# Gate/up bias of an expert as two 64-row products on the two row halves of the array

## The chip, the cores and the metric

The kernel runs on one core of a Trainium2 chip. The metric is the device time of one execution in microseconds (us), lower is better; the figure given for a kernel is the median of its runs.

## The reference

One layer of a decoder trunk is computed for 512 prompt tokens and 64 sample tokens (T = 576 in all): a combined input projection, a Mamba-2 branch, a latent attention branch, a gated merge, a layer norm, and then a mixture of 32 experts with the top 4 chosen for each token. The change lies in the experts:

```python
def expert_block(arg):
    xb, e = arg                                   # 128 rows of tokens, one expert
    gu = xb @ w_gu[e] + b_gu[e]                   # D_MODEL=1024 -> 2*D_FF=2048, gate and up interleaved
    g = jnp.minimum(gu[:, ::2], SWIGLU_LIMIT)
    u = jnp.clip(gu[:, 1::2], -SWIGLU_LIMIT, SWIGLU_LIMIT)
    h = (u + 1.0) * (g * jax.nn.sigmoid(SWIGLU_ALPHA * g))
    return h @ w_dn[e] + b_dn[e]
```

All inputs and outputs are float32.

## The kernel before

The program is a sequence of stages, each a block in which every engine has its own instruction list and engines meet through semaphores. `stage_choose` (up to about 1242 us of the profiled execution) does the output projection, the first layer norm and the routing. `stage_experts_combine` then runs the experts.

**An item** is one expert with up to 128 of its token rows. The first four items are written out, the others run in a loop of two per turn; a further loop for experts with more than 128 rows stands behind it and has nothing to do in the profiled execution. Each item reads 12 pieces of weights of 1 MiB (slots 0 to 3 for the first half of the gate/up matrix, 4 to 7 for its second half, 8 to 11 for the down matrix) into a ring of 8 raw buffers.

**Precision by splitting.** A float32 matrix is split into a high part in the type fp32r (ScalarE copies it, `high`, L2798) and a low part (VectorE subtracts, `low`, L2853). A product then needs three fp32r matmuls: x_hi by w_hi, x_hi by w_lo, x_lo by w_hi. `w_hi` and `w_lo` have 4 slots each. The order is: DMA brings a raw piece, ScalarE waits until TensorE has used the slot four pieces back (`w_used`) and writes `w_hi`, VectorE writes `w_lo`, TensorE uses both.

**TensorE's list in an item** (`run` in the tensor block). For each half h of the gate/up output: four pieces of 12 matmuls, all 128 rows by 128 columns with 512 moving columns (L2708), into PSUM banks 2h and 2h + 1, then `add_bias` (L2714), whose last matmul increments `gu_ready`. Then the down product, four more pieces, 48 matmuls. Between them stand 16 transposes (L2702) which turn the hidden rows and the token rows of the next item. So an item has 144 product matmuls, 4 bias matmuls and 16 transposes.

**The bias** is added by a matmul too. `pick[:, par, :]` is a one-hot over the experts, copied by GpSimd from column `K_PICK + e` of the constants and broadcast to 128 columns. `sb.b_all` is a table of 128 rows by 3072 columns: rows 0 to 31 hold the high parts of the biases of the 32 experts, rows 32 to 63 the low parts, rows 64 to 127 are zero in the gate/up columns 0 to 2047 (GpSimd writes them, L2161). One half needs two matmuls of 128 rows and 512 columns, one for each bank, with the same stationary operand. The down bias columns, with a second copy of the high part in rows 64 to 95, are used once at the very end (`down_bias`, L2771).

**After the bias** of a half ScalarE takes the sigmoid (L2807), VectorE clips and multiplies (L2862, L2863, L2866) and writes `hid`. TensorE needs the first half of `hid` for the transposes `turn(U_H0)`, behind the second piece of half 1, and the second half of it for `turn(U_H1)`, in the middle of the second piece of the down product.

**The set-up of the bias table** is in `stage_choose`: five DMAs of SyncE (L2130 to L2132) into the free room of `xT`, the up bias plus one on GpSimd (L2164), the high parts on ScalarE at the second token tile (L2327, L2328), the low parts on GpSimd (L2166).

Of the kernel before, what the change touches and what calls it, by code (L numbers as in the profile page):

```python
# [8 lines left out]
F32 = mybir.dt.float32  # L9
# [3 lines left out]
ALU = mybir.AluOpType  # L13
ACT = mybir.ActivationFunctionType
AX = mybir.AxisListType.X

P = 128
D = 1024
# [20 lines left out]
FF = 1024  # L39
E = 32  # L40
# [25 lines left out]
K_STRICT = K_TRI + P  # L66
# [15 lines left out]
K_PICK = K_VAL + NT  # L82
# [6 lines left out]
def constants():  # L89
    c = np.zeros((P, K_W), np.float32)  # L90
    r = np.arange(P)[:, None]
    q = np.arange(P)[None, :]
    c[:, K_ID:K_ID + P] = r == q
    c[:, K_TRI:K_TRI + P] = r <= q
    c[:, K_STRICT:K_STRICT + P] = r < q
    c[:, K_ONE:K_ONE + P] = 1
    c[:, K_CAUS:K_CAUS + P] = np.where(q <= r, 0, MASKED)
    l = np.arange(NS)
    same = l[:, None] // TS == l[None, :] // TS
    c[:NS, K_BTRI:K_BTRI + NS] = same & (l[:, None] <= l[None, :])  # L100
    c[:NS, K_BALL:K_BALL + NS] = same
    s = np.arange(NSEQ)
    c[:NS, K_BEND:K_BEND + NSEQ] = l[:, None] == s[None, :] * TS + TS - 1
    c[:NS, K_BROW:K_BROW + NSEQ] = l[:, None] // TS == s[None, :]
    c[:, K_BCOL:K_BCOL + NSEQ * NS] = (s[:, None] == l[None, :] // TS).reshape(1, -1)
    t = np.arange(TS)
    c[:, K_NEW:K_PAIR] = MASKED
    c[:HEADS * TS, K_NEW + NS - TS:K_NEW + NS] = np.where(t[None, :] <= np.tile(t, HEADS)[:, None], 0, MASKED)
    c[:, K_FOLD:K_FOLD + HEADS * TS] = r % (HEADS * TS) == np.arange(HEADS * TS)[None, :]
    c[:, K_SUB] = np.arange(P) % 16  # L110
    c[:NS, K_BMOD:K_BMOD + 4] = l[:, None] // TS % 4 == np.arange(4)[None, :]
    pair = np.zeros((P, NT * TOPK, 2))
    token = np.repeat(r + P * np.arange(NT)[None, :], TOPK, axis=1)
    pair[:, :, 0] = token
    c[:, K_PAIR:K_BASE] = pair.reshape(P, -1)
    c[:, K_BASE:K_BASE + E] = CAP * np.arange(E)
    c[:E, K_CODE:K_CODE + 4] = CAP * np.arange(E)[:, None] + P * np.arange(1, 5)[None, :]
    c[:E, K_CODE + 4] = np.arange(E)
    c[:, K_OVER:K_OVER + 4] = P * np.arange(1, 5)
    c[:, K_ITEM:K_ITEM + NOVF + 2] = np.arange(1, NOVF + 3)  # L120
    c[:, K_IOTA:K_IOTA + P] = q
    c[:, K_VAL:K_VAL + NT] = token[:, ::TOPK] - T
    c[:2 * E, K_PICK:K_PICK + E] = (r % E == np.arange(E)[None, :])[:2 * E]
    return c


# [1939 lines left out]
def stage_choose(nc, io, sb, sem):  # L2066

    with ExitStack() as ctx:
        buf = lambda n, s, d=F32: ctx.enter_context(nc.sbuf_tensor(n, s, d))
        K = sb.const  # L2070
        h, w_raw, w_hi, w_lo = sb.h, sb.w_raw, sb.w_hi, sb.w_lo
        room = sb.xT[:].rearrange("p k t -> p (k t)")
        b_raw = room[0:2 * E, 0:3 * D]
        down_again = room[2 * E:3 * E, 2 * D:3 * D]
        up = b_raw[:, 0:2 * FF].rearrange("p (f t) -> p f t", t=2)
        picks, parts = (room[:, 3 * D + 640 * j:3 * D + 640 * (j + 1)].rearrange("p (k i e) -> p k i e", k=TOPK, i=NT) for j in range(2))
        g_b, b_b = w_raw[4][:, 0, :], w_raw[4][:, 1, :]
        spots = w_raw[5].rearrange("p c n -> p (c n)")[:, 0:LISTED * NT * P].rearrange("p (e i c) -> p e i c", e=LISTED, i=NT)
# [38 lines left out]
        with nc.Block() as block:  # L2117
            @block.sync
            def _(sp):
                for q in (2, 3):  # L2120
                    sp.dma_start(w_out[q], out_piece(io, q)).then_inc(w_in_[q], 16)
                for i in range(NT):
                    sp.dma_start(h[0:ROWS[i], i, :], token_dram(io.xp, io.xs, i)).then_inc(x_in, 16)
                sp.dma_start(g_b, io.g1.broadcast_to((P, D))).then_inc(gb_in, 16)
                sp.dma_start(b_b, io.b1.broadcast_to((P, D))).then_inc(gb_in, 16)
                sp.dma_start(wr[:], io.wr.rearrange("(k p) n -> p k n", p=P)).then_inc(wr_in, 16)
                sp.dma_start(br[:], io.br.broadcast_to((P, E))).then_inc(wr_in, 16)
                sp.wait_ge(wo_low, 2)
                for p0 in (0, E):
                    sp.dma_start(b_raw[p0:p0 + E, 0:2 * FF], io.bgu).then_inc(b_in, 16)  # L2130
                    sp.dma_start(b_raw[p0:p0 + E, 2 * FF:3 * D], io.bdn).then_inc(b_in, 16)
                sp.dma_start(down_again, io.bdn).then_inc(b_in, 16)  # L2132
                sp.wait_ge(zeroed, 3)
                sp.dma_start(io.slots[NEMPTY:NEMPTY + P].unsqueeze(0), empty[0:1]).then_inc(cleared, 16)
                sp.dma_start(io.slots[0:NEMPTY].rearrange("(e j c) a -> e j c a", e=E, c=P),
                             empty[:].unsqueeze(1).broadcast_to((E, CAP // P, P, 2))).then_inc(cleared, 16)
                for rows in (io.y_sum, io.h_rows):
                    sp.dma_start(rows[T:T + P].rearrange("r (q n) -> r q n", n=ZW),
                                 zero.unsqueeze(1).broadcast_to((P, D // ZW, ZW))).then_inc(cleared, 16)
                for s in range(AHEAD):  # L2140
                    sp.wait_ge(wo_low, s + 1)
                    sp.dma_start(w_raw[s], weight_slot(io, 0, s)).then_inc(first_in[s], 16)
                for i in range(NT):
                    sp.wait_ge(done, i + 1)
                    sp.dma_start(io.h_rows[P * i:P * i + ROWS[i], :], h[0:ROWS[i], i, :]).then_inc(stored, 16)
                    sp.wait_ge(raised, i + 1)
                    sp.dma_start(io.y_sum[P * i:P * i + ROWS[i], :], stage[i % 2][0:ROWS[i], :]).then_inc(y_put[i % 2], 16)
                sp.wait_ge(stored, 16 * NT)
                sp.wait_ge(y_put[0], 48)
                sp.wait_ge(y_put[1], 32)  # L2150
                sp.wait_ge(cleared, 16 * 4)

            @block.gpsimd
            def _(pool):
                pool.memset(zero, 0.0).then_inc(zeroed, 1)
                pool.tensor_copy(sb.pair[:], K[:, K_PAIR:K_BASE].rearrange("p (n a) -> p n a", a=2)).then_inc(zeroed, 1)
                pool.memset(empty[:, :, 1], 0.0)
                pool.tensor_scalar(empty[:, :, 0], K[0:E, K_IOTA:K_IOTA + P], float(T), None, ALU.add).then_inc(zeroed, 1)
                pool.wait_ge(zeroed, 3)
                pool.wait_ge(wo_low, 4)  # L2160
                pool.tensor_copy(sb.b_all[2 * E:P, 0:2 * D], K[2 * E:P, K_STRICT:K_STRICT + 1].broadcast_to((P - 2 * E, 2 * D))).then_inc(b_low, 1)  # L2161
                pool.wait_ge(b_in, 80)
                pool.wait_ge(b_low, 1)
                pool.tensor_scalar(up[:, :, 1], up[:, :, 1], 1.0, None, ALU.add).then_inc(b_up, 1)  # L2164
                pool.wait_ge(b_high, 1)
                pool.tensor_tensor(sb.b_all[E:2 * E], b_raw[E:2 * E], sb.b_all[E:2 * E].bitcast(F32), ALU.subtract).then_inc(b_low, 1)  # L2166
                pool.wait_ge(b_low, 2)
                pool.wait_ge(stored, 16 * NT)
                pool.wait_ge(cleared, 16 * 4)
                pool.wait_ge(first_put, 1)  # L2170
                pool.indirect_dma_start(out=x_first, out_offset=None, in_=io.h_rows,
                                        in_offset=bass.IndirectOffsetOnAxis(ap=first_row[:].bitcast(U32), axis=0)).then_inc(x_got, 16)
                pool.wait_ge(x_got, 16)
# [96 lines left out]
            def _(act):  # L2270
# [42 lines left out]
                for i in range(NT):  # L2313
                    if i >= 1:
                        turned_copy(i - 1)
                    if i + 2 < NT:
                        act.wait_ge(mixed, i + 1)
                        merged_high(i + 2)
                    if i == NT - 1:
                        act.wait_ge(mixed, NT)  # L2320
                        expert_high(0)
                    root(i)
                    if i >= 1:
                        raise_rows(i - 1)
                    if i == 1:
                        act.wait_ge(b_up, 1)
                        act.activation(sb.b_all[2 * E:3 * E, 2 * D:3 * D], down_again, ACT.Copy)  # L2327
                        act.activation(sb.b_all[0:2 * E], b_raw, ACT.Copy).then_inc(b_high, 1)  # L2328
                expert_high(1)
                turned_copy(NT - 1)  # L2330
# [177 lines left out]
def stage_experts_combine(nc, io, sb):  # L2508
# [5 lines left out]
    with ExitStack() as ctx:  # L2514
        sem = ctx.enter_context(signals(nc, "experts"))
        buf = lambda n, s, d=F32: ctx.enter_context(nc.sbuf_tensor(n, s, d))
        K = sb.const
# [77 lines left out]
        with nc.Block() as block:  # L2595
# [102 lines left out]
            def _(pe):  # L2698
# [12 lines left out]

                def add_bias(par, bank, row, stop):
                    for c in range(2):
                        mm = pe.matmul(banks[:, bank + c, :], pick[:, par, :], sb.b_all[:, (row + c) * 512:(row + c + 1) * 512], start=False, stop=stop)  # L2714
                    return mm

                def run(it, par):
# [377 lines left out]
```

## Time and profile before

| | |
|---|---|
| median of 3 runs | 2427.85 us (2427.7 to 2431.04) |
| profiled execution | span 2428.8 us, its own time is this span |
| busy in it: TensorE matmul, weight load | 2315.2 us (95%), 1895.8 us (78%) |
| VectorE, ScalarE, GpSimd | 1845.1, 1341.9, 486.6 us |
| experts | from about 1242 us to 2395 us, 32 items |

The profile shows, for each engine, when each instruction started and how long it took; for a TensorE matmul the length includes the time in which it drains while the next is already under way, so the distance from one start to the next tells what a matmul costs in a stream. A group "x2" is two instructions in a row of the same line; its length runs from the first start to the last end.

### The profile page before, as it was taken

How to read it: one execution, taken by the hardware profiler on the slowest of the kernel's cores; microseconds unless marked ns; L12 is line 12 of the kernel's file. 1: busy time of each engine (PE TensorE's matmuls, PEld its weight loads, DVE VectorE, ACT ScalarE, POOL GpSimd, SP SyncE). 2: the span in 40 equal slices, each digit the busy share in tenths (PEclk: the TensorE clock that was granted, in tenths of full speed). 3: DMA queues.
4: the chain of work that ended last, by engine and by line, in shares of the span. 5: the costliest groups of instructions: out<-in, count | busy, mean ns of one | idle time of the engine just before them, and what ended most of it. 6: DMA issues, size and time to landing. Idle time of an engine off the chain costs nothing. (4 is left out here: it accounts for less than half of the span.)

```text
span 2428.8 us, 38736 instructions
## 1 busy us (share of the span) xinstructions
PE 2315.2 (95%) x14529; PEld 1895.8 (78%) x14529; DVE 1845.1 (76%) x2270; ACT 1341.9 (55%) x1470; POOL 486.6 (20%) x414
## 2 busy tenths in 40 slices
PE   8898999999989999998978999999999999999997
PEld 5486656999976667898767888888888888888885
DVE  2575556428778888444478999999999999999997
ACT  1351212314336776322337777777777777777775
POOL 0002220000014444000142222122122212212223
PEclk9997999999989999999979999999999999999999
DMA  5105562424232444433559999999999999999995
GB/s 174 67 1 201 188 218 99 122 54 154 83 86 78 143 133 111 148 122 112 182 165 362 394 394 397 392 382 381 395 382 379 389 391 380 378 395 384 380 386 195
DMA packets 250686, 593.64 MB, mean 244 GB/s; under 512 B 31056, under 2 KB 122577, under 8 KB 245836
## 3 DMA queue, kind: packets, MB, share of 16 engines
q1 hardware_dynamic: 232884, 514.07, 58.0%
q0 software_dynamic: 17680, 77.88, 10.1%
q8 instruction: 84, 1.38, 0.2%
q14 instruction: 38, 0.31, 0.0%
HBM read 553.75 MB, written 38.16 MB: 244 GB/s over the span
## 5 line engine op out<-in xcount | busy, mean ns | idle before, releaser
L2853 DVE TENSOR_TENSOR w_lo<-w_raw,w_hi 128x2048 fp32r<-128x2048 f32 x291 | 658.7, 2288 | 53.6 <-ACT w_hi L2798 49.6
L2798 ACT ACTIVATE w_hi<-w_raw 128x2048 fp32r<-128x2048 f32 x288 | 550.2, 1916 | 117.6 <-PE banks L2708 88.7
L2708 PE MATMUL banks<-w_hi,x_hi 128*128 128x512 f32 x1024 | 320.0, 394 | 3.9 <-DVEq L2898 3.5
L2708 PE MATMUL banks<-w_lo,x_hi 128*128 128x512 f32 x1024 | 316.9, 391 | 0.0
L2708 PE MATMUL banks<-w_hi,x_lo 128*128 128x512 f32 x1024 | 316.3, 390 | 0.0
L2853 DVE TENSOR_TENSOR w_lo<-mergedT,w_hi 128x2048 fp32r<-128x2048 f32 x96 | 220.0, 2292 | 33.1 <-ACT w_hi L2798 31.0
L2708 PEld LDWEIGHTS banks<-w_hi,x_lo 128*128 128x128 f32 x1024 | 192.8, 188 | 41.0
L2708 PEld LDWEIGHTS banks<-w_lo,x_hi 128*128 128x128 f32 x1024 | 192.9, 188 | 40.9
L2708 PEld LDWEIGHTS banks<-w_hi,x_hi 128*128 128x128 f32 x1024 | 190.5, 189 | 42.4 <-DVEq L2898 3.9
L2656 POOL DMA_INDIRECT y_sum<-xT,to_row x31 | 51.0, 1644 | 826.9 <-ACT xT L2835 783.6
L2798 ACT ACTIVATE w_hi<-mergedT 128x2048 fp32r<-128x2048 f32 x96 | 183.9, 1915 | 35.2 <-PE banks L2708 29.9
L2708 PE MATMUL banks<-w_hi,h_hi 128*128 128x512 f32 x512 | 161.6, 397 | 0.9 <-DVE w_lo L2853 0.9
L2708 PE MATMUL banks<-w_lo,h_hi 128*128 128x512 f32 x512 | 158.7, 391 | 0.0
L2708 PE MATMUL banks<-w_hi,h_lo 128*128 128x512 f32 x512 | 157.8, 389 | 0.0
L757 PE MATMUL banks<-keyT,q 32*64 32x256 f32 x2560 | 117.4, 424 | 17.0 <-issue 15.0
L757 PEld LDWEIGHTS banks<-keyT,q 32*64 32x64 f32 x2560 | 79.0, 148 | 49.9 <-issue 43.6
L2708 PEld LDWEIGHTS banks<-w_lo,h_hi 128*128 128x128 f32 x512 | 96.4, 188 | 20.7
L2708 PEld LDWEIGHTS banks<-w_hi,h_lo 128*128 128x128 f32 x512 | 96.2, 188 | 20.8
L2708 PEld LDWEIGHTS banks<-w_hi,h_hi 128*128 128x128 f32 x512 | 93.9, 189 | 19.0 <-DVE w_lo L2853 1.3
L808 ACT ACTIVATE prob<-banks,neg 128x1024 f32<-128x1024 f32 x16 | 17.8, 1114 | 155.9 <-DVE neg L856 155.9
L1175 DVE TENSOR_TENSOR ws_lo<-room,ws_hi 128x1024 fp32r<-128x1024 f32 x22 | 27.0, 1226 | 82.4 <-ACT ws_hi L1153 82.4
L1348 PE MATMUL banks<-xs_hi,ws_hi 128*128 128x288 f32 x384 | 84.3, 301 | 4.0 <-DVE ws_lo L1422 4.0
(539 smaller groups left out, 4743.4 us busy)
## 6 DMA issues: line engine op xcount, KB each, us to landing
w_raw<-in_exp_w_gu SPq DMA_DIRECT2D x196, 1024.0 KB
w_raw<-in_exp_w_down SPq DMA_DIRECT2D x96, 1024.0 KB, 9.8
mergedT<-in_exp_w_gu SPq DMA_DIRECT2D x64, 1024.0 KB
mergedT<-in_exp_w_down SPq DMA_DIRECT2D x32, 1024.0 KB, 9.8
w_x<-in_w_in SPq DMA_DIRECT2D x11, 1024.0 KB, 5.3
xT<-in_w_in SPq DMA_DIRECT2D x9, 1024.0 KB
room<-acs_rows SPq DMA_DIRECT2D x16, 512.0 KB, 4.0
mergedT<-in_state_ssm SPq DMA_DIRECT2D x16, 512.0 KB, 6.5
```

Of the source, the lines that this page charges most:

```text
L757: mm = pe.matmul(banks[64 * c:64 * (c + 1), i, 0:HALF], q4[at, b % 2, j, :], keyT[at, j, c * HALF:(c + 1) * HALF], start=(j == 0), stop=(j ...
L808: act.activation(prob[:, n % 2].rearrange("p (k i x) -> p i k x", k=BLK, i=4), scores_at.rearrange("p i (k x) -> p i k x", k=BLK), ACT.Exp ...
L1175: dve.tensor_tensor(w_lo[:, u % NW], w_raw[u % NR], w_hi[:, u % NW].bitcast(F32), ALU.subtract).then_inc(w_low, 1)
L1348: mm = pe.matmul(banks[:, b + piece, 0:H2], wp[:, c % 2, k, at:at + P], part[:, k, piece * H2:(piece + 1) * H2], start=(k == 0 and wp is w ...
L2656: pool.indirect_dma_start(out=io.y_sum, out_offset=bass.IndirectOffsetOnAxis(ap=to_row[:, par, :].bitcast(U32), axis=0), in_=y_out, in_off ...
L2708: mm = pe.matmul(banks[:, bank + c, :], x[:, k, :], part[:, s % NHI, j, c * 512:(c + 1) * 512], start=start, stop=last)
L2798: act.activation(w_hi[:, s % NHI], raw(s, par), ACT.Copy).then_inc(hi_ready, 1)
L2853: dve.tensor_tensor(w_lo[:, s % NHI], raw(s, par), w_hi[:, s % NHI].bitcast(F32), ALU.subtract).then_inc(lo_ready, 1)
```

## The change

The gate/up bias table is laid out a second time in rows 64 to 127 (rows 64 to 95 high, 96 to 127 low) where there were zeros. The one-hot column of the constants has the pattern in all 128 rows. The two bias matmuls of a half then take 64 rows each: the one for the first bank rows 0 to 63, the one for the second bank rows 64 to 127 of `pick` and of the table. In the set-up, two DMAs of 256 KB are added, the addition of one to the up bias goes over 128 partitions, ScalarE gets one more copy, GpSimd one more subtraction, and GpSimd's writing of zeros is gone.

```diff
-    c[:2 * E, K_PICK:K_PICK + E] = (r % E == np.arange(E)[None, :])[:2 * E]
+    c[:, K_PICK:K_PICK + E] = r % E == np.arange(E)[None, :]
...
         b_raw = room[0:2 * E, 0:3 * D]
+        gu_again = room[2 * E:P, 0:2 * D]
         down_again = room[2 * E:3 * E, 2 * D:3 * D]
-        up = b_raw[:, 0:2 * FF].rearrange("p (f t) -> p f t", t=2)
+        up = room[:, 0:2 * FF].rearrange("p (f t) -> p f t", t=2)
...
                     sp.dma_start(b_raw[p0:p0 + E, 2 * FF:3 * D], io.bdn).then_inc(b_in, 16)
+                for p0 in (2 * E, 3 * E):
+                    sp.dma_start(room[p0:p0 + E, 0:2 * FF], io.bgu).then_inc(b_in, 16)
                 sp.dma_start(down_again, io.bdn).then_inc(b_in, 16)
...
                 pool.wait_ge(zeroed, 3)
-                pool.wait_ge(wo_low, 4)
-                pool.tensor_copy(sb.b_all[2 * E:P, 0:2 * D], K[2 * E:P, K_STRICT:K_STRICT + 1].broadcast_to((P - 2 * E, 2 * D))).then_inc(b_low, 1)
-                pool.wait_ge(b_in, 80)
-                pool.wait_ge(b_low, 1)
+                pool.wait_ge(b_in, 112)
                 pool.tensor_scalar(up[:, :, 1], up[:, :, 1], 1.0, None, ALU.add).then_inc(b_up, 1)
                 pool.wait_ge(b_high, 1)
                 pool.tensor_tensor(sb.b_all[E:2 * E], b_raw[E:2 * E], sb.b_all[E:2 * E].bitcast(F32), ALU.subtract).then_inc(b_low, 1)
+                pool.tensor_tensor(sb.b_all[3 * E:P, 0:2 * D], room[3 * E:P, 0:2 * D], sb.b_all[3 * E:P, 0:2 * D].bitcast(F32), ALU.subtract).then_inc(b_low, 1)
...
                         act.activation(sb.b_all[2 * E:3 * E, 2 * D:3 * D], down_again, ACT.Copy)
+                        act.activation(sb.b_all[2 * E:P, 0:2 * D], gu_again, ACT.Copy)
                         act.activation(sb.b_all[0:2 * E], b_raw, ACT.Copy).then_inc(b_high, 1)
...
                 def add_bias(par, bank, row, stop):
                     for c in range(2):
-                        mm = pe.matmul(banks[:, bank + c, :], pick[:, par, :], sb.b_all[:, (row + c) * 512:(row + c + 1) * 512], start=False, stop=stop)
+                        at = slice(2 * E * c, 2 * E * (c + 1))
+                        mm = pe.matmul(banks[:, bank + c, :], pick[at, par, :], sb.b_all[at, (row + c) * 512:(row + c + 1) * 512], start=False, stop=stop)
                     return mm
```

## Rows read from the trace of the kernel before

**Rows 1.** The page: busy time by engine, share of the span, instructions.

```profile
PE 2315.2 (95%) x14529; PEld 1895.8 (78%) x14529; DVE 1845.1 (76%) x2270; ACT 1341.9 (55%) x1470; POOL 486.6 (20%) x414
```

**Rows 2.** The chain that ended last, in order of time: start, length, what.

```profile
1396.74 17.73 PE banks L2708 x78
...
1432.14 17.73 PE banks L2708 x78
...
2388.12 6.85 PE banks L2708 x30
```

**Rows 3.** One item by windows: length, busy time by engine, granted clock, DMA share, GB/s.

```profile
1432.14:1467.55 35.41, 35.41 (x166) 29.45 (x165) 33.13 (x23) 26.85 (x20) 7.29 (x6) 1.00 1.03 397
```

**Rows 4.** Waits from 1396.74 to 2388: who, for whom, total, times, longest.

```profile
ACT w_hi L2798 <- PE banks L2708: 108.3, 196, 0.8
...
DVE w_lo L2853 <- ACT w_hi L2798: 59.2, 83, 1.4
```

**Rows 5.** Timeline of PE around the bias of a half 0: start, length.

```profile
1449.26 0.62 PE L2708 MATMUL banks<-w_hi,x_lo 128*128 128x512 f32 x2
1449.71 0.61 PE L2714 MATMUL banks<-b_all,pick 128*128 128x512 f32 x2
1450.17 0.62 PE L2708 MATMUL banks<-w_hi,x_hi 128*128 128x512 f32 x2
```

**Rows 6.** Timeline of PE in the scan stage, 128-row fp32r matmuls before 32-row ones.

```profile
788.50 0.39 PE L1689 MATMUL banks<-ws_lo,xs_hi 128*128 128x512 f32 x1
788.73 0.40 PE L1689 MATMUL banks<-ws_hi,xs_lo 128*128 128x512 f32 x1
789.07 1.99 PE L1757 MATMUL banks<-b_of,xend 32*128 32x512 f32 x8
```

**Rows 7.** The same stage, from two pairs of 32-row matmuls back to 128 rows.

```profile
782.22 1.13 PE L1757 MATMUL banks<-b_of,xend 32*128 32x512 f32 x4
783.28 0.50 PE L1689 MATMUL banks<-ws_hi,xs_hi 128*128 128x512 f32 x1
783.62 0.39 PE L1689 MATMUL banks<-ws_lo,xs_hi 128*128 128x512 f32 x1
```

**Rows 8.** Line L1757's matmuls of the whole run: duration ns min/median/max, first and last start.

```profile
L1757 PE MATMUL banks<-b_of,xend x64: 587/587/692, 780.2 to 983.2; 32*128 32x512 f32 x64
```

**Rows 9.** Timeline of PE: four full float32 matmuls of 128 rows, 512 columns.

```profile
2402.46 1.88 PE L2784 MATMUL banks<-h,const 128*128 128x512 f32 x4
2404.18 0.59 PE L2789 MATMUL banks<-xT 128*128 128x512 f32 x1
```

**Rows 10.** Timeline of PE in the scan stage: 128 rows, then 64.

```profile
767.74 0.60 PE L1769 MATMUL banks<-const,y 128*128 128x128 f32 x4
768.26 1.14 PE L1701 MATMUL banks<-xdt,room 64*64 64x64 f32 x16
```

**Rows 11.** Timeline of PE in the third item: its half-1 bias and the turns.

```profile
1354.75 0.62 PE L2714 MATMUL banks<-b_all,pick 128*128 128x512 f32 x2
...
1360.30 1.09 PE L2702 MATMUL banks<-const,xT 128*128 128x128 f32 x8 [0.42 <-DMA xT<-h_rows,from_row]
```

**Rows 12.** Set-up, timeline of ACT.

```profile
1174.48 2.77 ACT L2328 ACTIVATE b_all<-xT 64x3072 fp32r<-64x3072 f32 x1
1179.65 0.60 ACT L2292 ACTIVATE mergedT<-banks 128x512 f32<-128x512 f32 x1 [2.40 <-PE banks L2198]
```

**Rows 13.** Set-up, timeline of POOL.

```profile
1163.69 3.33 POOL L2164 TENSOR_SCALAR xT<-xT 64x1024 f32<-64x1024 f32 x1 [9.04 <-DMA xT<-in_exp_b_down]
1177.34 6.79 POOL L2166 TENSOR_TENSOR b_all<-xT,b_all 32x3072 fp32r<-32x3072 f32 x1 [10.32 <-ACT b_all L2328]
1230.68 1.15 POOL L2171 DMA_INDIRECT xT<-h_rows,first_row  x1 [46.55 <-DVE first_row L2466]
```

**Rows 14.** The hidden rows' last step on DVE, and their turn on PE.

```profile
1464.50 0.69 DVE L2866 SCALAR_TENSOR_TENSOR xT<-xT 128x512 f32<-128x512 f32 x1
...
1466.08 1.47 PE L2702 MATMUL banks<-const,xT 128*128 128x128 f32 x12
```

## Prediction, before the changed kernel was run

> **What bounds the kernel now.** I read the busy times of the page first [rows 1]: TensorE works 95% of the span, the others less, so the question is whether its few gaps or its work set the end. The chain that ended last, in order of time, answers that for the experts [rows 2]: from about 1361 us to 2395 us it is TensorE alone, in pieces of product matmuls that come back every 35.40 us (1396.74, 1432.14). The window of one item shows the same from the other side [rows 3]: TensorE is busy 35.41 of 35.41 us at a granted clock of 1.00. VectorE has 2.3 us to spare in it, ScalarE 8.6. The DMA engines are busy throughout too (share 1.03, 397 GB/s), so it matters who waits for whom [rows 4]: in 28 items ScalarE waited for TensorE before its copies of weights (196 times, 108.3 us) and never for a weight transfer, TensorE for nobody. So a nanosecond more or less in TensorE's list of an item appears in the item, as long as DMA and VectorE keep up.
>
> The work in front is different. The third item waits for the gather of the fourth item's tokens until 1360.30 [rows 11]. Before it the first items wait for weights. So the stream that is bound by TensorE begins behind that turn and holds items 4 to 32: 29 items, 58 halves with a bias each.
>
> **What a bias costs now.** In the stream the last two product matmuls start from 1449.26, the two bias matmuls from 1449.71, the next two products from 1450.17 [rows 5]: 0.91 us for four starts, 0.227 us for each. A bias is two of these, 0.454 us.
>
> **What the change takes away.** Two 64-row matmuls on different row halves and into different banks can run side by side. The nearest row in the trace is line 1757 of the scan stage, pairs of 32-row matmuls in two row groups, into two banks, 512 columns each. Four of them (two pairs) start at 782.22 and the last ends 1.13 us later [rows 7]. Full float32 matmuls of 512 columns start every 0.43 us when they follow each other (2402.46 to 2404.18 is four) [rows 9], so four in a row would last 1.88. They went in pairs. By this row the change saves one of the two, 0.227 us in a half. That those are float32, which stream at 0.43 us and not 0.227, is the weak point of the analogy, and it is rival 2.
>
> **What the change adds.** The array goes from 128 rows to 64 and back, and the same line shows what that costs, in four places:
> - Before the first tiled matmul. Line 1689, fp32r, 128 rows, 512 columns, is the same kind as our products: its starts lie 0.23 apart (788.50, 788.73), but the first tiled one comes 0.34 behind the last (789.07) [rows 6]. That is +0.11.
> - In the first tiled pair. Line 1757's matmul lasts 587 ns in the median, 692 at most [rows 8], and the 1.13 us of rows 7 is 0.53 from the first pair to the second, not 0.43, and 0.59 or so. The weight load is not hidden under the matmul before. That is +0.105.
> - Behind the last tiled pair. From 782.22 to the next untiled start, 783.28, two pairs take 1.06 us [rows 7] instead of 0.86 (two times 0.43 [rows 9]). The excess of 0.20 holds the 0.105 just counted, so +0.095 remains.
> - In the first untiled matmul. It starts at 783.28, the next at 783.62: 0.34 instead of 0.23, and it lasts 0.50 instead of 0.39 [rows 7]. That is +0.105.
>
> Together 0.415 us for a visit to the tiled form. That 64 rows, and not only 32, are such a form is seen at line 1701: four 128-row transposes start at 767.74 and the 64-row matmul behind them at 768.26, 0.52 later [rows 10], where four at their usual 0.11 make 0.44. So the price of going in is paid there also.
>
> The Trainium skill has a rule against this change: "TensorEngine Tiling (Array Packing)", Tiling Modes, Key Properties, says that a change of the tiling mode drains TensorE. The trace agrees, with the 0.34 us above. The page "TensorE: Matmul & The Clock Gate", Part 3, tells the other half: matmuls of different row groups overlap almost entirely, with some 4 ns more for each tile. With that page alone the sum in a half would be a gain of 0.22 us; with both, a loss of the size of the drain less this.
>
> **The sum in a half.** Now, from the start of the last product to the start of the second product behind the bias: 4 times 0.227 = 0.91 us. Then: 0.227 + 0.11, the pair at 0.227 + 0.105 + 0.095, the first product at 0.227 + 0.105, which is 1.09 us. The difference is 0.415 - 0.227 = +0.19 us. Our products last 0.39 where the 788.73 one shows 0.40, so the drain may be a few ns less; I take +0.18. The rows' own spread (0.10 to 0.11 for each of four) gives 0.16 to 0.20.
>
> 58 halves by 0.18 us = +10.4 us.
>
> **What lies off the path.** The bias of the third item, half 1 (1354.75), is before the wait of 0.42 us for the gather [rows 11], which swallows 0.18. In half 0 of that item, and in the first two, TensorE's loss falls into waits for transfers and for VectorE. What hangs on the bias itself moves hardly at all: the last bias matmul ends at +0.11 + 0.105 - 0.227, about 0.01 us earlier than now, so the sigmoid, the gate and `hid` come when they do now, and the turn that needs `hid` comes later. The tighter of the two turns starts at 1466.08, its `hid` is ready at 1465.19 [rows 14]: 0.9 us of cover, which grows. SyncE's loads wait for freed buffers, so they get slower with TensorE and the DMA engines get relief, not load.
>
> The pick on GpSimd has the same shape as before and is ready long ahead.
>
> **The set-up.** ScalarE gets a copy of 64 by 2048. 64 by 3072 takes 2.77 us and ends at 1177.25 [rows 12], so the new one takes some 1.9. ScalarE then waits 2.40 us for TensorE, until 1179.65; it fits with 0.5 us over. Without this cover it would be at most 1.9 us. GpSimd's addition (3.33 us, from 1163.69) goes over 128 partitions, which I cost between 3.33 and twice that, and starts behind 512 KB more of transfers, 1.3 us at the 397 GB/s of rows 3; ScalarE wants it about a microsecond before 1174.48 [rows 12], so even 6.7 us fit. SyncE has two more issues in front of its list, of under a microsecond together; behind them stand the clearing of tables and the first expert's weights, whose users come tens of microseconds later. GpSimd's new subtraction of 32 by 2048 takes two thirds of 6.79 us, 4.5, and ends at about 1189; its next work is at 1230.68 [rows 13]. The zeros that it no longer writes were off the path. I cost the set-up at zero, at most 2 us.
>
> **The forecast.** The span of the profiled execution would go from 2428.8 to 2439.2 us. The runs' median is 2427.85, so 2438.3 us for the changed kernel.
>
> **Rivals.**
> 1. *The pair overlaps and the switch is free for our fp32r products*, for instance because weights of the next form are loaded while the last products stream. Then 58 times 0.227 = 13.2 us are gained: 2414.7 us. For it speaks that everything else in the stream hides its weight loads. This is also what the Trainium skill's page "TensorE: Matmul & The Clock Gate", Part 3, would give, which names no cost of a switch. Against it stands that the fp32r stream of line 1689 paid on both sides [rows 6, 7]. It decides from a switch of under 0.227 us. Chance 0.09.
> 2. *The pair does not overlap*, since two fp32r matmuls at 0.227 us each write two banks at twice the rate that any row here shows. Nothing is saved and the switch is paid: 58 times 0.415 = 24.1 us, 2451.9. Chance 0.10.
> 3. *The switch costs about what the pair saves*, 0.15 to 0.31 us, for instance with one of the four terms hidden. Then the time is within 5 us of before. Chance 0.08; the term that could go is the weight load of the first pair, which two 64-row loads might share otherwise than two 32-row ones.
> 4. *The forecast*: overlap and a full switch. Chance 0.73.
>
> **Range and chances.** This kernel's measurement can tell some 0.2%, 4.9 us. Rivals 2 and 4 are slower by more, 0.83; rival 3 is the same, 0.08; rival 1 faster, 0.09. The likeliest case by itself holds 2436 to 2441 us (0.16 to 0.20 in a half, and up to 2 us of set-up). The range that leaves out only rivals 1 and 3 is 2434 to 2452.
>
> **What the profile of the changed kernel would show.** The period of an item is 35.40 + 0.36 = 35.76 us, and TensorE is still busy all of it. The two bias matmuls start together, within 0.01 us; they last about 0.49 and not 0.39 us. The last product before them is followed 0.33 us later by the pair, the pair 0.42 us later by a product, and that product, 0.50 us long, 0.33 us later by the next. If the pair starts 0.2 us apart, rival 2 holds; if a product of 0.39 us follows the pair after 0.23, rival 1. The experts begin at 1242 us as now. The prediction is wrong if the switch of a 64-row form into whole-column width is cheaper than that of line 1757, if the pair is serial, or if TensorE's loss is caught up by a wait that I have not seen; rows 4 show none.

## The result, and the profile of the changed kernel

The changed kernel takes 2439.68 us in the median of 5 runs (2435.6 to 2443.45), the kernel before 2428.84 us in 5 runs (2427.7 to 2431.04). The ratio is 1.004 with a 95% interval of 1.0029 to 1.0052: slower by 10.8 us (7 to 13 by the interval). The profiled execution has a span of 2436.1 us and a time of 2438.17. The profile says where the loss is: in TensorE's list, at every bias.

The chain that ended last, in order of time (start, length, what), for two items of the changed kernel; it answers to [rows 2]:

```profile
1426.85 17.73 PE banks L2710 x78
1444.58 0.43 PE banks L2717 x2
1445.01 5.67 PE banks L2710 x24
...
1456.61 0.43 PE banks L2717 x2
1457.04 4.31 PE banks L2710 x18
1461.35 1.31 PE banks L2704 x12
1462.66 17.73 PE banks L2710 x78
...
1498.48 17.73 PE banks L2710 x78
...
2393.81 6.85 PE banks L2710 x30
```

It is still TensorE from end to end. Line 2710 is the product (2708 before), 2717 the bias, 2704 the transposes. An item takes 35.81 us (1426.85 to 1462.66 to 1498.48, and to 2393.81 in the mean of 27 items), where it took 35.41 (1396.74 to 2388.12 is 28): +0.41, 0.20 for each bias. One item by windows (length, busy time by engine, granted clock, DMA share, GB/s), and who waited for whom from 1390 to 2390 (total, times, longest), beside [rows 3, 4]:

```profile
1462.66:1498.48 35.82, 35.82 (x166) 28.91 (x165) 33.19 (x23) 26.84 (x20) 7.27 (x6) 1.00 1.03 394
```

```profile
ACT w_hi L2801 <- PE banks L2710: 120.0, 195, 0.8
...
DVE w_lo L2856 <- ACT w_hi L2801: 66.2, 84, 1.4
```

TensorE is busy for all of the 35.82 us at the same clock, no weight transfer is waited for, and ScalarE waits longer for TensorE than before (120.0 us, not 108.3; the window is 9 us longer). "Busy" therefore hides the loss: the starts move apart while a matmul is always on record. The records of the weight loads (PEld) changed: they fell from 29.45 to 28.91 us in an item that got longer, mostly since the two loads of a pair now run side by side.

The timeline of TensorE around one bias of half 0 shows the terms of the loss; it answers to [rows 5]:

```profile
1443.51 0.62 PE L2710 MATMUL banks<-w_lo,x_hi 128*128 128x512 f32 x2
1443.97 0.61 PE L2710 MATMUL banks<-w_hi,x_lo 128*128 128x512 f32 x2
1444.51 0.50 PE L2717 MATMUL banks<-b_all,pick 64*128 64x512 f32 x2
1444.94 0.73 PE L2710 MATMUL banks<-w_hi,x_hi 128*128 128x512 f32 x2
1445.52 0.62 PE L2710 MATMUL banks<-w_lo,x_hi 128*128 128x512 f32 x2
```

The weight loads of the same stretch:

```profile
1444.51 0.19 PEld L2717 LDWEIGHTS banks<-b_all,pick 64*128 64x128 f32 x2 [0.35 <-issue]
1444.94 0.30 PEld L2710 LDWEIGHTS banks<-w_hi,x_hi 128*128 128x128 f32 x2 [0.24 <-issue]
```

Two products from 1443.97 take 0.54 us until the pair starts, not 0.45. The pair's two matmuls lie on top of each other: 0.50 us from the first start to the last end, and each lasts 0.498. The next product comes 0.43 us behind the pair's start, and from it to the third product behind the pair it is 0.58 us, not 0.45. So 0.54 + 0.43 + 0.58 = 1.55 us stand where 6 starts of 0.227, 1.36 us, stood. That is 0.19 us; some 0.01 more comes in the starts behind it. The loads of the pair, both within 0.19 us, start with the pair itself at 1444.51 after 0.35 us without a load, and those of the next products at 1444.94 after 0.24; in the untiled stream a load lies under the matmul before it. That the rest of the gap is the array running empty (draining) before its form changes is read into the distances and has no row of its own.

The set-up is hidden. ScalarE's and GpSimd's timelines, beside [rows 12, 13]:

```profile
1169.72 1.89 ACT L2329 ACTIVATE b_all<-xT 64x2048 fp32r<-64x2048 f32 x1
1171.63 2.77 ACT L2330 ACTIVATE b_all<-xT 64x3072 fp32r<-64x3072 f32 x1
1175.00 1.09 ACT L2293 ACTIVATE mergedT<-banks 128x512 f32<-128x512 f32 x2 [0.60 <-PE banks L2199]
```

```profile
1161.38 3.58 POOL L2164 TENSOR_SCALAR xT<-xT 128x1024 f32<-128x1024 f32 x1 [25.97 <-DMA xT<-in_exp_b_down]
1174.48 6.79 POOL L2166 TENSOR_TENSOR b_all<-xT,b_all 32x3072 fp32r<-32x3072 f32 x1 [9.52 <-ACT b_all L2330]
1181.35 5.49 POOL L2167 TENSOR_TENSOR b_all<-xT,b_all 32x2048 fp32r<-32x2048 f32 x1
1226.03 1.15 POOL L2172 DMA_INDIRECT xT<-h_rows,first_row  x1 [39.19 <-DVE first_row L2468]
```

ScalarE still waits 0.60 us for TensorE behind its new copy, and GpSimd's next work comes 39 us after its new subtraction.

**From span to span.** The two profiled executions differ by 7.3 us and not by 11. From the first bias product to the last they take 1125.30 and 1135.90 us, +10.6; from there to the down bias +0.3; the part in front of the first bias was 5.3 us shorter (1251.79 and 1257.04) and the part from the down bias on 1.6 us longer (32.89 and 31.27). The last two are not the change's: over the eight profiles of this study the first bias starts anywhere from 1247.7 to 1257.0, and the length of the end goes with TensorE's granted clock in the 12.5 us behind the down bias's start. The end is 31.3 us where that clock is 1.00 (before, and the run with four visits), 32.9 us where it is 0.86 (the changed kernel twice, and three others), 34.2 us where it is 0.75 (the run with one visit).

### The profile page after: what moved, and what is told of

It reads as the page before. It is cut to its first block and busy times, and to the rows that moved or that the text cites. A ratio compares the mean times of both kernels' runs of the same rounds, so it can differ in the third digit from the quotient of the medians.

```text
span 2436.1 us, 38738 instructions
## 1 busy us (share of the span) xinstructions
PE 2324.2 (95%) x14529; PEld 1875.2 (77%) x14529; DVE 1850.3 (76%) x2270; ACT 1344.1 (55%) x1471; POOL 494.7 (20%) x414
```

## The experiments

The expected times start from 2429 us. The kernel before took 2424.43 us in the runs beside the first three experiments (one chip) and 2429.48 beside the last three (another chip), so each experiment is compared with the kernel before beside it. The period is the time from one item to the next. "Theory A" is the explanation of the prediction: each visit to the 64-row form costs 0.43 us, and a product that runs beside another costs nothing.

### The set-up alone

The changed kernel's set-up, with the one-hot and the bias products of before.

```diff
-    c[:, K_PICK:K_PICK + E] = r % E == np.arange(E)[None, :]
+    c[:2 * E, K_PICK:K_PICK + E] = (r % E == np.arange(E)[None, :])[:2 * E]
...
-                        at = slice(2 * E * c, 2 * E * (c + 1))
-                        mm = pe.matmul(banks[:, bank + c, :], pick[at, par, :], sb.b_all[at, ...
+                        mm = pe.matmul(banks[:, bank + c, :], pick[:, par, :], sb.b_all[:, ...
```

> The new set-up of the bias table (two more DMAs, the extra copy and subtraction) with the bias products and the one-hot of before: two products over 128 rows; the one-hot is zero in rows 64 to 127, so the second layout adds nothing. Theory A (the whole loss is TensorE's switch between 128-row and 64-row form, 0.43 us a visit, less 0.227 us for the overlap of the pair): the set-up hides, 2429 us within 2 us, an item period of 35.41 us. Rival B (part of the +10.8 us is the set-up: a later first load of weights or a longer ScalarE list): 2 to 10 us slower than before, with the period unchanged.

Measured: 2423.29 us in the median (before: 2424.43), ratio 0.9994 (0.9983 to 1.0006). One item by windows:

```profile
1426.00:1461.41 35.41, 35.41 (x167) 29.45 (x165) 33.13 (x23) 26.85 (x20) 7.29 (x6) 1.00 1.03 396
```

The chain has the same period of 35.41 us. The set-up costs nothing that can be measured: by the interval at most 1.5 us, where B had 2 to 10. B falls.

### Both products on the same row half

The kernel before, with 64 rows in both products.

```diff
-mm = pe.matmul(banks[:, bank + c, :], pick[:, par, :], sb.b_all[:, ...
+mm = pe.matmul(banks[:, bank + c, :], pick[0:2 * E, par, :], sb.b_all[0:2 * E, ...
```

> The kernel before, but both bias products take rows 0 to 63 alone (the rows from 64 on hold zeros, so nothing is lost): 64-row form, both on the same row half. Theory A: the switch is paid (0.43 us a visit, 58 visits that count) and nothing overlaps, +25 us, 2454 us; the two products start 0.227 us apart; period 35.41 + 0.86 = 36.27 us. Rival C (in the changed kernel the pair did not really run side by side, the records only say so): the time of the changed kernel, 2440 us, period 35.81 us.

Measured: 2450.74 us (before: 2424.43), ratio 1.0087 (1.0058 to 1.0116). That is +26.3 us, where A had +25 and C +11. There are only four runs, from 2437.44 to 2452.68, and the interval, +14 to +28 us, lies just above C, so the time alone is coarse; the timeline and the chain in order of time are not:

```profile
1445.76 0.61 PE L2708 MATMUL banks<-w_hi,x_lo 128*128 128x512 f32 x2
1446.30 0.73 PE L2714 MATMUL banks<-b_all,pick 64*128 64x512 f32 x2
1446.96 0.73 PE L2708 MATMUL banks<-w_hi,x_hi 128*128 128x512 f32 x2
1447.53 0.62 PE L2708 MATMUL banks<-w_lo,x_hi 128*128 128x512 f32 x2
```

```profile
1428.64 17.73 PE banks L2708 x78
...
1464.90 17.73 PE banks L2708 x78
```

The period is 36.26 us, 0.85 over before: 0.43 for each visit, as A had it (36.27). The way in (0.54 us from 1445.76) and the way out (0.57 from 1446.96) are those of the changed kernel; only the pair differs, 0.66 us to the next product and not 0.43. That 0.23 us is the overlap, and C falls. A detail of A was wrong: the two products do not start 0.227 apart. The pair is 0.73 us long and its last matmul is 0.39, so the second starts 0.34 behind the first. The weight loads:

```profile
1446.30 0.29 PEld L2714 LDWEIGHTS banks<-b_all,pick 64*128 64x128 f32 x2 [0.35 <-issue]
```

The records of both weight loads lie within 0.29 us from 1446.30, the pair's own start. So it is the first product's load that is not hidden; the second's lies under the first product.

### 96 rows

```diff
-mm = pe.matmul(banks[:, bank + c, :], pick[:, par, :], sb.b_all[:, ...
+mm = pe.matmul(banks[:, bank + c, :], pick[0:3 * E, par, :], sb.b_all[0:3 * E, ...
```

> The kernel before, but both bias products take rows 0 to 95 (rows 64 to 95 hold zeros). Theory A (what costs is the change of the array's form, and 96 rows cannot be a half or a quarter): the same as before, 2429 us, period 35.41 us, products 0.227 us apart. Rival D (any product over fewer than 128 rows pays for the change of row count): +25 us as for rows 0 to 63.

Measured: 2428.29 us (before: 2424.43), ratio 1.0014 (1.0002 to 1.0025), +3.9 us where A had none and D 25.

```profile
1439.37 0.63 PE L2714 MATMUL banks<-b_all,pick 96*128 96x512 f32 x2
1439.84 0.63 PE L2708 MATMUL banks<-w_hi,x_hi 128*128 128x512 f32 x2
1440.31 0.62 PE L2708 MATMUL banks<-w_lo,x_hi 128*128 128x512 f32 x2
1440.77 0.63 PE L2708 MATMUL banks<-w_hi,x_lo 128*128 128x512 f32 x2
```

```profile
1421.80 17.73 PE banks L2708 x78
...
1457.33 17.73 PE banks L2708 x78
```

No start in front is late and no load is exposed: D falls, its 25 us being some seven times what was measured. But A's "the same" is not quite right either. Two starts take 0.47 us at the bias and for two products behind it, not 0.45, and the period is 35.53: 0.12 us in an item, 3.5 us over 29 items, which agrees with the runs. What stretches these starts by some ns each was not looked into.

### One visit in an item

Half 1's pair follows half 0's in the same visit, and opens the sum of its banks.

```diff
-                def add_bias(par, bank, row, stop):
+                def add_bias(par, bank, row, start, stop):
...
-mm = products(4 * h + q, j, x_hi, x_lo, 2 * q + j, 2 * h, q == 0 and j == 0)
+mm = products(4 * h + q, j, x_hi, x_lo, 2 * q + j, 2 * h, h == 0 and q == 0 and j == 0, h == 1 and q == 3 and j == 1)
...
                         if h == 0:
                             pe.wait_ge(picked, it + 1)
-                        add_bias(par, 2 * h, 2 * h, True).then_inc(gu_ready, 1)
+                            add_bias(par, 0, 0, False, True).then_inc(gu_ready, 1)
+                            pe.wait_ge(gu_read, it * 2 + 2)
+                            add_bias(par, 2, 2, True, False)
...
-                    act.wait_ge(gu_ready, it * 2 + h + 1)
+                    act.wait_ge(*((gu_ready, it + 1), (w_used, it * NW + NW + 8))[h])
```

> The changed kernel with the two visits of an item to the 64-row form joined in one: behind half 0's products, its pair of bias products and then the pair of half 1, which opens the sum in banks 2 and 3; half 1's last product closes it. Theory A (the switch is paid per visit, a pair in the form costs 0.227 us more): per item 0.43 + 2 x 0.227 - 4 x 0.227 = -0.02 us, 29 items: -0.7 us, 2428 us, period 35.39 us. Rival E (the cost is one of each tiled pair, not of the visit): as the changed kernel, 2440 us, period 35.81 us.

Measured: 2428.44 us (before: 2429.48), ratio 0.9997 (0.9986 to 1.0008). The timeline and the chain:

```profile
1443.26 0.61 PE L2710 MATMUL banks<-w_hi,x_lo 128*128 128x512 f32 x2
1443.80 0.73 PE L2717 MATMUL banks<-b_all,pick 64*128 64x512 f32 x4
1444.46 0.73 PE L2710 MATMUL banks<-w_hi,x_hi 128*128 128x512 f32 x2
```

```profile
1426.16 17.71 PE banks L2710 x78
...
1461.53 17.74 PE banks L2710 x78
...
1496.93 17.73 PE banks L2710 x78
```

Four bias products take the same 0.66 us as the two serial ones of the run on the same half, and the period is 35.39 (1426.16 to 1496.93 is two). Half of the visits gone, all of the loss gone, and nothing more: A is right to 0.01 us, and E, which had 2440 us, falls. This version does not beat the kernel before; it equals it.

### Four visits in an item

Each 64-row product stands alone, six products apart.

```diff
                             for j in range(2):
+                                if q == 3 and j == 1:
+                                    if h == 0:
+                                        pe.wait_ge(picked, it + 1)
+                                    add_bias(par, 2 * h, 2 * h, False, (0,))
...
-                        if h == 0:
-                            pe.wait_ge(picked, it + 1)
-                        add_bias(par, 2 * h, 2 * h, True).then_inc(gu_ready, 1)
+                        add_bias(par, 2 * h, 2 * h, True, (1,)).then_inc(gu_ready, 1)
```

> The changed kernel with each pair split: the 64-row product of the first bank goes in front of the last piece-half's six products, that of the second bank stays behind them. Twice the visits (four in an item), no pair, same products. Theory A: nothing overlaps and each visit is paid, 4 x 0.43 = 1.72 us more in an item, 29 items: +50 us, 2479 us, period 37.1 us. Rival E (a cost of the tiled product, not of the visit): four such products without overlap cost what two such pairs cost and 0.45 us more, +25 us, 2454 us.

Measured: 2479.86 us (before: 2429.48), ratio 1.0207 (1.0187 to 1.0227).

```profile
1449.12 0.61 PE L2710 MATMUL banks<-w_hi,x_lo 128*128 128x512 f32 x2
1449.67 0.50 PE L2717 MATMUL banks<-b_all,pick 64*128 64x512 f32 x1
1450.10 0.72 PE L2710 MATMUL banks<-w_hi,x_hi 128*128 128x512 f32 x2
1450.66 0.61 PE L2710 MATMUL banks<-w_lo,x_hi 128*128 128x512 f32 x2
1451.11 0.61 PE L2710 MATMUL banks<-w_hi,x_lo 128*128 128x512 f32 x2
```

```profile
1433.37 16.37 PE banks L2710 x72
...
1470.49 16.37 PE banks L2710 x72
```

The period is 37.12 us in this item and 37.13 in the mean of 28, 1.72 over before, four times 0.43; +50.4 us of medians where A had 50 and E 25. The 0.43 is a mean of the visits: the first of a half, shown here, costs 0.40 us, since the starts behind it are back at 0.45 for two from 1450.66 on, and the second, with wider starts behind it, 0.46. A single 64-row product takes 0.43 us to the next start (0.42 in the second visit), as the pair did. So the second product of a pair is free to within 0.01 us, and all of the cost is the visit.

### The changed kernel again

> The changed kernel once more beside the two others on the same chip. Theory A: 0.20 us in each of 58 halves, +11.8 us over before less what the run-to-run spread of the stages in front gives or takes: 2439 to 2441 us, period 35.81 us.

Measured: 2442.04 us (before: 2429.48), ratio 1.0053 (1.0038 to 1.0067). That is +12.6 us (9 to 16 by the interval), and the time lies 1 us above the range that was expected, 2439 to 2441. The period is again 35.81 us in the trace.

Put side by side, the extra time in an item is visits times 0.43 us, less 0.227 for each product that runs beside another. The 0.43 was taken from the changed kernel (0.20 + 0.227), so the other three rows are its tests:

| kernel | visits | hidden products | worked out, us | measured period less 35.41, us |
|---|---|---|---|---|
| same half | 2 | 0 | 0.86 | 0.85 |
| changed | 2 | 2 | 0.41 | 0.41 |
| one visit | 1 | 2 | -0.02 | -0.02 |
| four visits | 4 | 0 | 1.72 | 1.72 |

## Why the prediction was right

- **TensorE alone bounds the items behind the third, and a change of its list appears in each.** Right. From the fourth item on the period stays within 0.03 us of its mean in every kernel here. The run with four visits shows that also a much larger change is neither caught up nor made worse.
- **The pair overlaps.** Right, shown by the run on the same half: 0.66 us without overlap, 0.43 with it, from the pair's start to the next product's. These are distances between starts; the ends of matmuls in the profile are modelled. The weak point named, that the row in the trace streams float32 at half the rate, did not matter. Rival 2, the serial pair, is refuted. The Trainium skill, "TensorE: Matmul & The Clock Gate", Part 3, has such tiles some 4 ns apart, and here a pair of matmuls of 0.498 us takes 0.50 us together.
- **The switch is paid at four places, 0.415 us.** Right in kind, a little small. The starts in the trace, in the mean over 27 items, give in ns: going in 92 (forecast 110); in and behind the pair 204 (200, as 105 + 95); the first product behind it 111 (105); the next few starts together 23 (nothing). That is 430 and not 415, so 0.20 us in a half. The way in was forecast too large, and the wider starts behind the first product are the term that was left out. The prediction then rounded its own 0.19 down to 0.18. The band it gave, 0.16 to 0.20, does not follow from its terms either: four of 0.10 to 0.11, less 0.227, are 0.17 to 0.21; and 58 times 0.16 lead to 2437 us, not 2436.
- **What the price is made of.** The run on the same half separates the two drains from the two loads. Its second product, whose load is hidden, needs 0.32 us to the next 128-row product (0.66 - 0.34), which is 0.095 over 0.227. So the drain that the Trainium skill's "TensorEngine Tiling (Array Packing)", Key Properties, announces is the 0.09 us in front and as much behind; it is less than half of the price. The weight load that is not hidden on either side is nearly all of the rest. The two drains alone, 0.19 us, would have been paid for by the 0.227 saved.
- **58 halves.** 29 items at 0.408 us are 11.8 us; from first to last bias the profiles differ by 10.6. Of the 1.2 us between, 0.8 lies in the first three items, which wait for transfers and which took that much less in the changed kernel's profile than in the other, and 0.3 in the wait for the gather; the last visit's way out lies behind the last bias. The wait for the gather, in the third item, forecast to swallow its half-1 loss, went from 0.42 to 0.16 us:

```profile
1354.14 1.09 PE L2704 MATMUL banks<-const,xT 128*128 128x128 f32 x8 [0.16 <-DMA xT<-h_rows,from_row]
```

- **What hangs on the bias does not move.** Right. The tighter turn had 0.9 us of cover [rows 14] and has 1.1 now:

```profile
1459.41 0.69 DVE L2869 SCALAR_TENSOR_TENSOR xT<-xT 128x512 f32<-128x512 f32 x1
```

```profile
1461.19 1.04 PE L2704 MATMUL banks<-const,xT 128*128 128x128 f32 x8
```

- **The set-up is hidden.** Right, shown by the run with the set-up alone. GpSimd's new subtraction took 5.49 us and not 4.5, and the addition over 128 partitions 3.58 us, next to the lower of the two bounds; both are covered.
- **The base.** The prediction took the span of the profiled execution as its time. The two are not the same: in every later run of either kernel the time is 1.7 to 2.4 us above the span, and none of the three runs behind 2427.85 took 2428.8. As the sum was made on the median of the runs, this did not enter.
- **Rivals 1 and 3**, a free or a half-priced switch, are refuted by the same rows and by the table above.
- **The signs named in advance** came: a period of 35.81 us (forecast 35.76), a pair together of 0.50 us (0.49), and starts of 0.32, 0.43 and 0.34 us (0.33, 0.42, 0.33).

The forecast was 2438.3 us, measured were 2439.68. That the two are so close is in part luck. The item's period says +11.8 us for the whole stream, where the forecast had +10.4. The medians said +10.8 the first time and +12.6 the second, with the spread of the other stages in them.

## What to carry to other kernels

In a stream that TensorE bounds, a visit to a row-tiled form and back costs about 0.43 us here, nearly the time of two 512-column fp32r products, and what it saves is one product (0.227 us) for each that runs beside another. So a visit must hide at least two products before it breaks even; one pair loses, two pairs come out even. More than two pairs in a visit, or more than two row groups, were not run. Before tiling a small product in the middle of a stream, look in the trace for any line that already goes tiled, read the start distances on both sides of it, and multiply by the visits and not by the products.

## What was not expected of the hardware

- A product over 96 rows is not a switch, but neither free: 0.06 us for each bias of two such products, 0.12 us in an item. The starts around it are 0.47 us for two and not 0.45.
- Two tiled products on the same row half, or two pairs behind each other in one visit, share one exposed weight load: 0.66 us to the next 128-row product, where a single product or pair takes 0.43. The further pair costs 0.23 us.
- Behind most visits the products do not return to 0.227 us at once. In the changed kernel the next four or five starts are 2 to 9 ns wider, 0.02 us together. This does not belong to the tiled form: behind the first visit of a half in the run with four visits it is absent, and the kernel before has it behind its 12 transposes, with no tiled product near (0.47 us for two starts from 1467.85). What causes it stays open.

```profile
1467.31 0.71 PE L2708 MATMUL banks<-w_hi,h_hi 128*128 128x512 f32 x2
1467.85 0.63 PE L2708 MATMUL banks<-w_lo,h_hi 128*128 128x512 f32 x2
1468.32 0.62 PE L2708 MATMUL banks<-w_hi,h_lo 128*128 128x512 f32 x2
```
